# Low halves of the weights on VectorE alone, borrowed PSUM banks and other first units in a two-layer decoder trunk

## The reference

```
u = rms_norm(h, norm_mix) @ w_in                  # 1024 -> 3092 columns, cut among four head groups
h = h + concat[SSD(u), Retention(u), GLA(u), RG-LRU(u)] @ w_out
hn = rms_norm(h, norm_ffn)
h = h + (silu(hn @ w_gate) * (hn @ w_up)) @ w_down            # 2816 hidden columns
```

## Time and profile before

| | |
|---|---|
| median of three runs | 1504.34 us |
| the profiled execution | 1504.16 us |
| its span, first to last instruction | 1502.4 us |
| PE, PEld busy | 1434.0 us (95%), 1377.9 us (92%) |
| VectorE busy | 733.1 us (49%) |
| ScalarE busy | 463.9 us (31%) |
| GpSimd busy | 392.3 us (26%) |
| low halves on GpSimd | 163 of 128 x 1024, 2406 ns each |
| low halves on VectorE | 44 of the same shape, 1311 ns each |

### The profile page before, as it was taken

How to read it: one execution, slowest core, us unless ns; L and a number is a source line. 1 busy time by engine, 2 the same in 40 slices (tenths; PEclk the granted TensorE clock), 3 DMA queues, 4 the chain that set the end, 5 groups by cost and what they waited for, 6 DMA issues and landing times.

```text
span 1502.4 us, 26368 instructions
## 1 busy us (share of the span) xinstructions
PE 1434.0 (95%) x11490; PEld 1377.9 (92%) x11490; DVE 733.1 (49%) x1313; ACT 463.9 (31%) x622; POOL 392.3 (26%) x167
## 2 busy tenths in 40 slices
PE   6999999999999999999989998999999999999995
PEld 5888889899999999999978887889999999999994
DVE  5855767454431233133758556763633213422347
ACT  5514224333221222122533151434322222222233
POOL 1000000243433443334500000003333334433443
PEclk8998989899999999999999998989999999999997
DMA  6212221132223222322322122122222322223232
GB/s 221 63 51 78 78 68 43 61 98 71 85 88 96 85 85 85 95 89 85 113 70 77 49 85 70 55 74 71 71 85 86 94 88 85 85 89 95 85 99 102
DMA packets 35730, 125.96 MB, mean 84 GB/s; under 512 B 4512, under 2 KB 5536, under 8 KB 35488
## 3 DMA queue, kind: packets, MB, share of 16 engines
q1 hardware_dynamic: 30672, 112.72, 24.0%
q10 hardware_dynamic: 4944, 11.57, 2.4%
HBM read 116.22 MB, written 5.82 MB: 81 GB/s over the span
## 4 chain that ended last, share of the span: by engine, by line
PE 79%; DVE 13%; DVEq 3%; ACT 2%; issue 1%; DMA 1%; ACTq 0%
PE bank L1165 69%; DVE sq_sum L639 3%; DVE wl L1051 1%; PE bank L1126 1%; DVE xl L644 1%; DVE ct L698 1%; PE bank L1357 1%; DVE h L1065 1%; PE bank L1241 1%; DVEq L638 1%; PE bank L1379 1%; PE bank L1137 1%; PE bank L1313 0%; PE bank L1246 0%; PE bank L1367 0%
## 5 line engine op out<-in xcount | busy, mean ns | idle before, releaser
L1165 PE MATMUL bank<-xh,wh 128*128 128x272 f32 x2208 | 660.2, 299 | 25.3 <-DVE xl L654 8.8
L361 POOL TENSOR_TENSOR wl<-raw,wh 128x1024 fp32r<-128x1024 f32 x163 | 392.1, 2406 | 1094.1 <-ACT wh L382 709.6
L1165 PE MATMUL bank<-xh,wl 128*128 128x272 f32 x2208 | 650.5, 295 | 0.0
L1165 PE MATMUL bank<-xl,wh 128*128 128x272 f32 x2208 | 647.2, 293 | 0.0
L1165 PEld LDWEIGHTS bank<-xh,wh 128*128 128x128 f32 x2208 | 428.4, 194 | 39.7 <-issue 23.4
L1165 PEld LDWEIGHTS bank<-xl,wh 128*128 128x128 f32 x2208 | 429.4, 194 | 0.7
L1165 PEld LDWEIGHTS bank<-xh,wl 128*128 128x128 f32 x2208 | 427.4, 194 | 0.0
L390 ACT ACTIVATE wh<-raw 128x1024 fp32r<-128x1024 f32 x96 | 101.8, 1060 | 432.0 <-PE bank L1165 432.0
L1085 DVE TENSOR_TENSOR tz<-bank,rs_bcast 128x272 f32<-128x272 f32 x176 | 77.5, 441 | 299.7 <-PE bank L1165 295.9
L382 ACT ACTIVATE wh<-raw 128x1024 fp32r<-128x1024 f32 x108 | 114.2, 1058 | 295.4 <-PE bank L1165 289.7
L1106 DVE TENSOR_TENSOR h<-h,bank 128x272 f32<-128x272 f32 x64 | 27.8, 438 | 150.1 <-PE bank L1165 150.1
(11 more groups left out here) (307 smaller groups left out, 1901.6 us busy)
## 6 DMA issues: line engine op xcount, KB each, us to landing
raw<-weights SPq DMA_DIRECT2D x207, 512.0 KB, 3.5
h<-x ACTq DMA_DIRECT2D x4, 544.0 KB, 6.3
y<-h SPq DMA_DIRECT2D x4, 544.0 KB, 2.7
cs<-consts SPq DMA_DIRECT2D x1, 1597.5 KB, 8.7
rv<-rk ACTq DMA_DIRECT2D x8, 136.0 KB, 2.4
tz<-rq ACTq DMA_DIRECT2D x8, 136.0 KB, 2.4
S<-s_ssd ACTq DMA_DIRECT2D x2, 512.0 KB, 4.3
n_ssd<-Vx ACTq DMA_DIRECT2D x2, 512.0 KB, 3.0
```

The source lines that it names most:

```text
L361: nc.gpsimd.tensor_tensor(wl[:, s, :], raw[:, s, :], wh[:, s, :].bitcast(F32), ALU.subtract).then_inc(lo_done, 1)
L1165: ins = mm(bank_, wt[:, slot, w], xx[:, cols], start=(i == 0 and j == 0), stop=(i == len(ks) - 1 and j == 2))
```

## The change

- **Low halves.** All 202 are subtracted on VectorE, in program order by one function; GpSimd has no work of its own. SyncE's loads, written as a loop, wait for the one semaphore that is left.
- **Padding.** There is no padding unit; a layer has 101 units, and nothing is loaded past the last one.
- **Borrowed banks.** Halves 3 and 4 of a layer, and the same two after the first FFN unit (q = 2 FFN0 + 3 and + 4), go to the mixers' banks M[2] and M[3] and wait for no `dense` bank.
- **First units.** The first unit of each part runs both halves over seven K-tiles, then the square sums, then both halves of the last K-tile (in layer 0 the first unit alternates its halves at every K-tile, and the sums come after unit 1). The spreading of the RMS factor comes after one more half.
- **Last squares.** Only tiles 0 to 6 are added up on VectorE; TensorE adds the square of tile 7 to its sum from `sq` by five more products (`last_squares`).
- **The rest.** The stage `dt` goes from slot 3 to slot 5. The loads of x are issued by SyncE, that of unit 2 ahead of the constants; VectorE makes the column of ones itself. The final norm makes no xh and xl. The sample chunk is transposed as the others are.

```diff
--- before.py
+++ after.py
-ON_VECTOR = range(3, NIN)
...
+BORROWED = {2 * u + 3 + i: 2 + i for u in (0, FFN0) for i in range(2)}
...
-at_slot(3, "dt")
+at_slot(5, "dt")
 at_slot(6, "gla_gate")
...
+        def dense_bank(layer, q):
+            return (M[BORROWED[q]] if q in BORROWED else dense[(layer * (2 * NUNIT) + q) % 3])[:, 0:HALF]
         def by_sequence(cols):
...
             sp.dma_start(raw[:, 0, :], weights[0]).then_inc(raw_loaded[0], 16)
+            for i in range(KT // 2):
+                sp.dma_start(h[:, 2 * i:2 * i + 2, :], x[:, 2 * i:2 * i + 2, :]).then_inc(x_loaded[i], 16)
             sp.wait_ge(x_loaded[1], 16)
...
             sp.wait_ge(x_loaded[KT // 2 - 1], 16)
+            sp.dma_start(raw[:, 2, :], weights[2]).then_inc(raw_loaded[2], 16)
             sp.dma_start(S1[:, 0:NEXACT], consts[:, NCONST + KT:NCONST + KT + NEXACT]).then_inc(exact_loaded, 16)
+            sp.wait_ge(lo_done, 1)
+            sp.dma_start(raw[:, 0, :], weights[3]).then_inc(raw_loaded[0], 16)
             sp.dma_start(cs[:], consts[:, 0:NCONST]).then_inc(consts_loaded, 16)
...
+            for u in range(1, RING):
+                sp.wait_ge(lo_done, u + 1)
+                sp.dma_start(raw[:, u, :], weights[u + RING]).then_inc(raw_loaded[u], 16)
+            with sp.Fori(1, ALL // RING - 1) as turn:
+                for s in range(RING):
+                    sp.wait_ge(lo_done, turn * RING + (s + 1))
+                    sp.dma_start(raw[:, s, :], weights[turn * RING + (s + RING)]).then_inc(raw_loaded[s], 16)
+            for u in range(ALL // RING * RING, ALL):
...
-        @block.gpsimd
-        def _(pool):
-            def split(s, n):
-                pool.wait_ge(hi_done, n + 1)
-                nc.gpsimd.tensor_tensor(wl[:, s, :], raw[:, s, :], wh[:, s, :].bitcast(F32),
...
+            def split(n):
+                if n < ALL:
+                    dve.wait_ge(hi_done, n + 1)
+                    tt(wl[:, n % RING, :], raw[:, n % RING, :], wh[:, n % RING, :].bitcast(F32),
+                       ALU.subtract).then_inc(lo_done, 1)
...
             def add_squares(m):
-                if m:
+                if 0 < m < KT - 1:
                     dve.drain()
                     tt(sq_sum[:], sq_sum[:], sq[:, m % 2, :], ALU.add).then_inc(sq_added.sem, 1)
             def xl_tile(layer, i, m, gain):
                 dve.wait_ge(h_squared.sem, h_squared.at(layer, i * KT + m + 1))
+                if (layer, i) == (DEPTH - 1, 1):
+                    return add_squares(m)
...
                 dve.wait_ge(x_rounded, m + 1)
                 stt(xl[:, m, :], h[:, m, :], tz[:, 0, m:m + 1], xh[:, m, :].bitcast(F32), ALU.mult,
                     ALU.subtract).then_inc(xl_done.sem, 1)
-            for m in range(1, KT):
+            for m in range(1, KT - 1):
                 dve.wait_ge(h_squared.sem, m + 1)
                 add_squares(m)
+                if m % 3 == 0:
+                    split(m // 3)
             dve.wait_ge(exact_loaded, 16)
...
-                    if s % 2 and s // 2 + 2 in ON_VECTOR:
-                        split(s // 2 + 2)
+                    if s % 2 and (s > 1 or layer):
+                        split(layer * NUNIT + s // 2 + 2)
...
+                            split(layer * NUNIT + u0 + m + 2)
                         if m:
                             xl_tile(layer, i, m - 1, par(gain, m - 1))
                     xl_tile(layer, i, KT - 1, par(gain, KT - 1))
+                    split(layer * NUNIT + u0 + KT + 1)
                     rms_rstd(layer, i)
                 new_h(0, OUT0, "norm_ffn")
...
                         tt(tz[:, i // 2, cols], acc, rs_bcast[:, cols], ALU.mult).then_inc(dense_free.sem, 1)
                         if i == 1:
                             dve.drain().then_inc(gate_out.sem, 1)
+                            split(layer * NUNIT + u0 + 2)
                     dve.drain()
                     dve.wait_ge(gate_silu.sem, count)
                     tt(tz[:, 1, :], tz[:, 1, :], tz[:, 0, :], ALU.mult).then_inc(act_out.sem, 1)
                     dve.wait_ge(act_hi.sem, count)
                     hi, lo = operand(j)
                     tt(lo, tz[:, 1, :], hi.bitcast(F32), ALU.subtract).then_inc(act_lo.sem, 1)
+                    split(layer * NUNIT + u0 + 3)
...
+                pe.wait_ge(sq_added.sem, sq_added.at(layer, (i + 1) * (KT - 2)))
                 for c, off, n in CH:
-                    ins = mm(M[4][0:n, c:c + 1], sq_sum[:, off:off + n], cst("ones"), start=True, stop=True)
+                    mm(M[4][0:n, c:c + 1], sq_sum[:, off:off + n], ones[:], start=(c == 0), stop=False, skip_group_check=True)
+            def last_squares(layer, i):
+                pe.wait_ge(h_squared.sem, h_squared.at(layer, (i + 1) * KT))
+                for c, off, n in CH:
+                    ins = mm(M[4][0:n, c:c + 1], sq[:, (KT - 1) % 2, off:off + n], ones[:], start=False, stop=True,
+                             skip_group_check=True)
                 ins.then_inc(stat_done.sem, 1)
...
+                        if q not in BORROWED:
+                            pe.wait_ge(dense_free.sem, dense_free.at(layer, q + 1 - 3))
+                        if half == 0:
+                            pe.wait_ge(lo_done, n + 1)
+                    cols = slice(half * HALF, (half + 1) * HALF)
+                    bank_ = dense_bank(layer, q)
...
                 for s in range(2 * NIN):
-                    def operand_ready(k, s=s):
-                        if s == 0:
-                            pe.wait_ge(xl_done.sem, xl_done.at(layer, k + 1 - KT))
-                    unit_half(s // 2, s % 2, x_operand, range(KT), operand_ready)
-                    if s == 1:
-                        pe.wait_ge(consts_loaded, 16)
+                    def operand_ready(k):
+                        pe.wait_ge(xl_done.sem, xl_done.at(layer, k + 1 - KT))
+                    if s > 1:
+                        unit_half(s // 2, s % 2, x_operand, range(KT))
+                    elif s == 1 and layer == 0:
+                        for k in range(KT):
+                            for half in range(2):
+                                unit_half(0, half, x_operand, range(KT), operand_ready, range(k, k + 1))
+                    elif s == 1:
+                        for half in range(2):
+                            unit_half(0, half, x_operand, range(KT), operand_ready, range(KT - 1))
+                        square_sums(layer, -1)
+                        last_squares(layer, -1)
+                        for half in range(2):
+                            unit_half(0, half, x_operand, range(KT), operand_ready, range(KT - 1, KT))
+                    if (s, layer) == (3, 0):
+                        square_sums(layer, -1)
+                        last_squares(layer, -1)
                         pe.wait_ge(exact_done, 1)
-                        square_sums(layer, -1)
-                    if s == 2:
+                    if s == (2 if layer else 4):
                         spread_rstd(layer, -1)
...
                     pe.wait_ge(xl_done.sem, xl_done.at(layer, k + 1))
-                unit_half(FFN0, 0, x_operand, range(KT), norm_ready)
+                for half in range(2):
+                    unit_half(FFN0, half, x_operand, range(KT), norm_ready, range(KT - 1))
                 square_sums(layer, 0)
-                unit_half(FFN0, 1, x_operand, range(KT))
+                last_squares(layer, 0)
+                for half in range(2):
+                    unit_half(FFN0, half, x_operand, range(KT), norm_ready, range(KT - 1, KT))
+                unit_half(FFN0 + 1, 0, x_operand, range(KT))
                 spread_rstd(layer, 0)
```

More of the change, by code:

```diff
@@ L612, in _ @@
                         next_operand(layer, 1, i - 2 * REST, lambda m: par("norm_next", m))
-                for i in range(PAD):
-                    hi_ahead(layer, NUNIT + i)
                 root(layer, 1)
@@ L1502, in _ @@
+                    for i in range(2 * n + 1, 2 * n + KT):
+                        for half in range(2):
+                            unit_half(first + i, half, operand, range(n))
             square_sums(DEPTH, -1)
+            last_squares(DEPTH, -1)
             spread_rstd(DEPTH, -1)
```

161 lines of the change are left out of this document (58 added, 103 removed).

## The result

The changed kernel takes 1484.68 us (median of four runs, 1482.2 to 1486.29) against 1504.57 us for the kernel before on the same chip; the ratio is 0.9865, with a 95% interval of 0.985 to 0.9881. The forecast was 1479 us with a range of 1470 to 1490. A second set of four runs, beside the first experiments, gave 1484.06 us and 0.9858 [0.9838, 0.9878].

What follows compares the result with a forecast made beforehand. TensorE was taken to bound nearly everything, with losses at the norms and ends. Terms 4.2 + 4.9 + 3.3 + 6.6 + 1.0 + 6.0 - 0.6 = 25.4 us off 1504.2 gave 1479 us, range 1470 to 1490.

Steps and rivals of the forecast that it cites:

- What bounds the kernel: TensorE bounds nearly everything (79% of the chain, VectorE 13%); losses lie at norms, layer change, start and end.
- The low halves cost nothing in the FFN: FFN pairs: VectorE's weight low half comes 3.9 us after the pair, TensorE is busy until 6.04 us, so no wait.
- Rival D: FFN pairs: the weights' low half comes too late and TensorE waits at every pair; 1523 us, chance 0.04.
- Additions at 0.73 us: Norms: without GpSimd's subtractions, VectorE's `sq_sum` additions take about 0.73 us everywhere, where the median was 2.74.
- rival C: Norms: GpSimd is not what slows `sq_sum`; additions stay at 2.75 us, costing 24 us; 1503 us, chance 0.03.
- w_out to FFN, +4.9 and +3.3: Norm before each FFN: overhead falls to 3.1 us, gaining 4.9 us in layer 0 and 3.3 in layer 1.
- Change of layers, +6.6: Between layers: 3.0 us overhead for 10.5, then waits of 1.7 and 1.9 us before halves 9 and 10; gain 6.6 us.
- Rival A: Norms: the clock falls behind the short sum products, losing 2.0 to 2.6 us at each of four; 1489 us, chance 0.13.
- Start, +4.2: Program start: copies 0.9 us earlier, two VectorE waits gone, up to 2.7 us lost if the clock falls; gain 4.2 us.
- slow half units "of the mixers": Mixers: some slow-clock half units, 2 us each, might fall elsewhere; counted only toward the range's lower end of 1470 us.
- End, +6.0: After the last product: sums start about 1.5 us later in place of 7.92 idle; gain 6.0 us, out of 4.5 to 7.5.
- Rival B: Layer heads: VectorE's first conv slots eat the gains, leaving 2 us at start, 3 at layer change; 1485 us, chance 0.07.

Runs made afterwards that it cites:

- gp_back: The changed kernel with the low halves of all units but 3 to 24 of a layer back on GpSimd; 1481.28 us, ratio 0.9834.
- after_again: The changed kernel, unedited, run and profiled a second time beside the first experiments; 1484.06 us, ratio 0.9858 to the kernel before.
- no_first: The changed kernel with the first unit's old order (half 0, sums, half 1) from w_out to FFN and at the change of layers; 1490.67 us.
- early_low: The changed kernel with VectorE's low half made before a convolution's taps and half 9 in a borrowed bank; 1476.75 us, ratio 0.9807.
- gp_no_last: gp_back with all eight squares added on VectorE, none on TensorE; 1480.12 us, ratio 0.9826.
- gp_no_first: The changed kernel with no_first's old order and the low halves of all units but 3 to 24 on GpSimd; 1498.08 us, ratio 0.9944.
- after: The first profiled execution of the changed kernel, whose median is 1484.68 us, ratio 0.9865 to the kernel before.
- dve_only: The kernel before with all low halves on VectorE and nothing else of the change; 1486.44 us, ratio 0.987.
- no_last: The changed kernel with all eight squares added on VectorE, so one set of ten sum products per norm; 1477.19 us, ratio 0.9815.
- no_borrow: The changed kernel without borrowed banks; in layer 0 sums and spreading come earlier again; 1489.1 us, ratio 0.9886.
- gp_early: gp_back with early_low's two edits at the layer heads; 1478.52 us, ratio 0.9814.
- early_ends: early_low with TensorE's last squares kept only at the start and the end; 1475.38 us, ratio 0.9805.
- early_none: early_low with all eight squares added on VectorE at every norm; 1472.11 us, ratio 0.978.

## Why the prediction was right, and where it was not

- **What bounds the kernel.** Right: the gain lies at the norms and the ends, and the FFN gave 0.6 us a layer.
- **The low halves cost nothing in the FFN.** Right: TensorE is busy for 382.00 of 382.00 us. Rival D is out.
- **Additions at 0.73 us.** Right (724 to 729 ns), so rival C is out. But the kernel did not need it: gp_back keeps slow additions and is no slower, with 0.75 us lost in each FFN. (The 24 us of rival C stay untested: in gp_back VectorE has no low halves to make beside the slow additions of a norm.) The prediction treated the terms as parts of a sum that needs both; they are two covers of one wait, each nearly enough alone.
- **w_out to FFN, +4.9 and +3.3.** Measured 4.8 and 3.2. The overhead forecast at 3.1 us is 2.7, since TensorE waits for nothing behind the spreading.
- **Change of layers, +6.6.** Measured 3.4 (3.6 in after_again), and this is the step that failed: the term takes full clock behind the sums and behind the second wait. Its two waits are there (1.20 and 1.86 us where 1.7 and 1.9 stood), so the order of events was right, though the first is for a bank and not for `wl`; the clock was not. The low clock behind the sums costs 1.52 us, and again 1.48 us behind the second wait, by the same pieces of gp_back, which has neither fall. It shows the step without the falls:

```profile
748.73 1.14 PE bank L1146 x10
749.86 3.98 PE bank L1176 x30
...
781.59 9.31 PE bank L1176 x72
```

  Its stretch takes 49.86 us, 6.75 less than before, the size that was forecast. (The terms that the prediction prints for it, 7.5 less 1.7 and 1.9 and plus 1.86, make 5.8 us and not 6.6; the first wait came out about 0.6 us shorter.) Rival A is thus right in part: the clock falls at one norm of three inside, not at all of them, and costs 1.5 us and not 2.0 to 2.6; but there it also delays VectorE's chain. The row that spoke against A was of another kind than the text says: those 20 products have two columns each (128x2).
- **Start, +4.2.** Measured 6.0 (4.75 in after_again). The half unit behind the sums kept full clock, the upper end of that term, and TensorE idled 1.11 us before unit 1 where 1.7 was taken. The clock is luck here: no_first and early_low run the same program up to that point, and there the next 24 matmuls take 4.64 and 4.56 us in place of 3.11. The lower gain in after_again has such a cause as well: behind the wait of 1.86 us half 10 takes 4.62 us there, and 3.10 in the first profiled run. The chain of the kernel before, then of the kernel after:

```profile
23.85 5.74 PE bank L1165 x24
```

```profile
22.90 0.94 PE bank L1128 x10
23.83 1.14 PE bank L1133 x10
24.97 3.21 PE bank L1163 x24
```

- **No term for the first state products.** They lose 3.0 and 2.7 us behind waits of 1.79 and 1.85 us, where the kernel before waited 1.78 and 2.12 us and lost nothing. The prediction kept some slow half units "of the mixers" for the range alone, as a gain. Together with the change of layers (3.2 short) this makes 8.9 us; the start, the rest of the mixers and the end gave 1.8, 3.2 and 0.5 us more than forecast. That leaves 22.0 of 25.4 us (w_out to FFN and the FFN make up the rounding): misses of 8.9 us one way and 5.5 the other, so that the time came out this near is in part luck. The profiled execution took 1482.2 us; the median of 1484.7 lies 2.5 us above it, within the spread of the clock (below).
- **End, +6.0.** Measured 6.5, with the sums at 1.47 us. The number was right; that the padding and an unused operand, not the last squares, carry it, is what gp_no_last added.
- **Rival B** is out: the waits did not grow beyond the forecast. VectorE does bound the head of a layer, though, as early_low shows.

The Trainium skill ("TensorE: Matmul & The Clock Gate", Part 1) says that the throttled clock is the default state and that activity lifts it. The granted clock of 0.50 behind the short products agrees where a wait came before them (no_first, gp_no_first) and once where none did (after, 744.77); the other two norms of the changed kernel, with 20 short products and no wait, kept full clock. The Trainium skill ("SBUF — State Buffer", Who interferes with whom) says that a VectorE instruction with two inputs in SBUF contends with a GpSimd instruction that reads SBUF. The additions agree: 2.74 us beside GpSimd's subtractions in gp_back, 0.73 us in the kernel without them.

**Open.** Why the clock falls behind the first state products' wait isn't settled. Half 12 to 16 takes 26.6 to 26.7 us in both layers of the changed kernel and of the seven runs that leave VectorE's taps and low halves there in their old order (16 of 16), behind waits of 1.79 to 1.86 us, against 23.60 and 23.93 before, behind 1.78 and 2.12. dve_only takes 27.07 in layer 0 but 23.60 in layer 1, with waits of 2.16 and 1.77 us. So the length of the wait does not decide it, and no run changed that wait by itself.

For the other falls the traces show at least that the program alone does not decide. In the changed kernel and those seven runs the wait before half 10 is 1.85 to 1.87 us in both layers; half 10 takes 4.6 us behind it in 10 cases of 16 and 3.1 in 6. And the twenty products of one column that a stage of the mixers makes in every kernel (line 1401 of the changed kernel), with no wait ahead of them, are followed by 24 matmuls in 5.32 us in the first profiled run of the changed kernel and in 3.30 in after_again. The table by stage, 3.30 us from the first of these matmuls on in after, then in after_again:

```profile
228.28:231.58 3.30, 3.30 (x22) 3.30 (x20) 3.02 (x6) 2.33 (x4) 0.00 (x0) 0.69 0.02 5
```

```profile
232.00:235.30 3.30, 3.29 (x27) 3.07 (x24) 3.08 (x7) 1.94 (x2) 0.00 (x0) 1.00 0.23 45
```

Whether the fall at one norm of three in the changed kernel is of that kind is not shown: after, after_again and early_low all have it at the change of layers and none has it from w_out to the FFN. What it hangs on stays open.

## What to carry to other kernels

Two edits that hide the same wait are not worth their sum: try each alone and drop the one that costs work on the bounding engine, as TensorE's second set of sums did here. Price a wait of TensorE with the half unit that may run at half the clock behind it (1.5 us here, in some executions and not in others), and look whether an engine's chain waits for that half unit. Before crediting a gain at the end of a program to the main edit, look what useless work beside it the edit also removed. And before crediting a few microseconds between two profiled runs to an edit, look whether the clock fell in one of them where the edit does not reach.

## What the runs showed beyond this

- One kernel's runs spread with the clock: no_last took 1470.86 us at a mean granted clock of 0.973 and 1480.28 us at 0.963, gp_no_last 1469.67 us at 0.975 and 1481.0 at 0.966. Differences of 3 us between kernels here are within that spread.
- At the three norms inside, behind twenty short products, the clock fell in 6 of 6 cases where the first unit was held up first (by 0.58 us in no_first, by 2.33 in gp_no_first), and without a wait in 3 of 18: at the change of layers in after, after_again and early_low, not in gp_back, no_borrow or gp_early, and never from w_out to the FFN. Behind ten products it fell in none of 15 (no_last, gp_no_last, early_ends, early_none, dve_only), in spite of waits of 0.52 and 0.56 us in gp_no_last and 0.58 to 0.72 in dve_only. The kernel before, with ten products behind waits of 2.33 us, did lose there: the next 24 matmuls take 5.61 and 4.38 us from w_out to the FFN, where 3.1 is full clock.
- The place of the low halves does show in the FFN: 376.57 to 376.59 us a layer in the four kernels with GpSimd's subtractions and the new bank plan, 375.67 to 375.82 in all that have them on VectorE (376.44 in the kernel before). TensorE waits 0.5 us once per layer there, for an operand of VectorE's.
